# A decoder step on one core: rotary rows exchanged by small transfers, the spread of the sample gates two tiles later, small cache moves issued in other stages

## The reference, cut to what matters

```
mod = silu(c) @ w_ada + b_ada             # six shift / scale / gate vectors
h = rmsnorm(x) * (1 + scale1) + shift1
q, k, v, gates, q_dil, k_dil, v_dil, merge gates = split(h @ w_in)
rotate(x): first quarter of a head, half = d // 8
    out = [x1*cos - x2*sin, x2*cos + x1*sin, rest]     # x1, x2: its two halves
o_nsa = g0*compressed + g1*selected + g2*window attention
o_dil = three dilated groups, mixed by softmax weights
m = sigmoid(gA) * (o_nsa @ w_bn) + sigmoid(gB) * (o_dil @ w_bd)
x = x + gate1 * (m @ w_out)
x = x + gate2 * (silu(h2@w_gate) * (h2@w_up)) @ w_down
y = rmsnorm(x)
```

## Time and profile before

| what | value |
|---|---|
| median of three runs | 2079.82 us |
| the profiled execution | 2076.5 us, span 2074.7 us |
| PE busy | 1929.0 us, 93% of the span |
| DVE, ACT busy | 976.7 us, 772.7 us |
| granted TensorE clock, mean | 0.964 of full speed |
| DMA | 512.54 MB, mean 247 GB/s |
| chain that ended last | PE 84%, DMA 9%, DVE 4%, ACT 3% |

### The profile page before, as it was taken

The page is one execution under the profiler, slowest core; times in us unless marked ns, Lnnn a source line. Parts: engine busy times, 40 slices in busy tenths (PEclk is TensorE's granted clock), DMA queues, the critical chain, the costliest instruction groups (busy, mean ns, idle before and its releaser), DMA issues.

```text
span 2074.7 us, 36811 instructions
## 1 busy us (share of the span) xinstructions
PE 1929.0 (93%) x15765; PEld 1774.5 (86%) x15765; DVE 976.7 (47%) x1730; ACT 772.7 (37%) x1232; POOL 58.4 (3%) x108
## 2 busy tenths in 40 slices
PE   6988999999999987899999978999999999999967
PEld 3667999999755555799999968999999999999966
DVE  3355445554355532355445764444444333745424
ACT  2355333334344432443334334333333332633322
POOL 0000000000000000000000000000000000000010
PEclk9998989999999989799999989999999999999989
DMA  9981769899899855755656545676777766677791
GB/s 373 422 304 62 213 209 304 270 294 284 328 420 420 324 233 202 266 169 178 186 176 214 182 163 182 231 271 229 253 252 244 241 232 215 208 252 245 262 320 49
DMA packets 336138, 512.54 MB, mean 247 GB/s; under 512 B 8753, under 2 KB 310105, under 8 KB 319497
## 3 DMA queue, kind: packets, MB, share of 16 engines
q1 hardware_dynamic: 316146, 368.53, 53.0%
q0 software_dynamic: 5248, 125.73, 15.3%
q10 hardware_dynamic: 14640, 16.80, 2.5%
HBM read 504.29 MB, written 98.91 MB: 291 GB/s over the span
## 4 chain that ended last, share of the span: by engine, by line
PE 84%; DMA 9%; DVE 4%; ACT 3%; issue 1%; SPq 0%; DVEq 0%; ACTq 0%
PE bank L1132 18%; PE bank L1134 18%; PE bank L1133 18%; PE bank L845 5%; PE bank L846 5%; PE bank L847 5%; DMA piece<-in_w_ada 5%; PE bank L735 3%; PE bank L772 2%; DMA piece<-in_w_down 2%; PE bank L903 1%; DMA mem<-in_cache_sel_kv,runs 1%; PE bank L963 1%; PE bank L878 1%; PE bank L800 1%; DMA mem<-in_x_sample 1%
## 5 line engine op out<-in xcount | busy, mean ns | idle before, releaser
L1132 PE MATMUL bank<-piece,piece 128*128 128x264 f32 x3072 | 878.3, 286 | 49.3 <-DVE piece L2054 26.5
L1133 PE MATMUL bank<-piece,piece 128*128 128x264 f32 x3072 | 877.7, 286 | 0.0
L1134 PE MATMUL bank<-piece,piece 128*128 128x264 f32 x3072 | 877.4, 286 | 0.0
L2059 DVE TENSOR_TENSOR piece<-piece,piece 128x2048 fp32r<-128x2048 f32 (+2 forms) x216 | 440.8, 2053 | 504.0 <-ACT piece L1544 504.0
L1132 PEld LDWEIGHTS bank<-piece,piece 128*128 128x128 f32 x3072 | 583.2, 190 | 50.3 <-DVE piece L2059 22.7
L1544 ACT CAST piece<-piece 128x2048 fp32r<-128x2048 f32 (+2 forms) x216 | 368.8, 1715 | 588.3 <-PE bank L1134 509.6
L1134 PEld LDWEIGHTS bank<-piece,piece 128*128 128x128 f32 x3072 | 583.1, 190 | 0.0
L1133 PEld LDWEIGHTS bank<-piece,piece 128*128 128x128 f32 x3072 | 582.6, 190 | 0.0
L845 PE MATMUL bank<-piece,piece 128*128 128x264 f32 (+1 forms) x816 | 240.8, 295 | 0.0
L846 PE MATMUL bank<-piece,piece 128*128 128x264 f32 (+1 forms) x816 | 234.8, 288 | 0.0
L847 PE MATMUL bank<-piece,piece 128*128 128x264 f32 (+1 forms) x816 | 234.5, 287 | 0.0
(11 more groups left out here) (324 smaller groups left out, 1417.5 us busy)
## 6 DMA issues: line engine op xcount, KB each, us to landing
piece<-in_w_ada SPq DMA_DIRECT2D x48, 2048.0 KB, 12.9
out_s_dil<-in_cache_dil_kv POOLq DMA_DIRECT2D x64, 1023.5 KB, 6.2
piece<-in_w_in SPq DMA_DIRECT2D x50, 1024.0 KB, 8.1
piece<-in_w_gate SPq DMA_DIRECT2D x22, 2048.0 KB, 8.1
piece<-in_w_up SPq DMA_DIRECT2D x22, 2048.0 KB, 8.2
piece<-in_w_down SPq DMA_DIRECT2D x32, 1408.0 KB, 7.2
piece<-in_w_in SPq DMA_DIRECT2D x16, 2048.0 KB, 8.2
piece<-in_w_out SPq DMA_DIRECT2D x8, 2048.0 KB, 8.6
```

The source lines that it names most:

```text
L1132: mm(out, w_high[:, k, :], half_tile(x_high[k]), start=(start and k == first_tile), stop=False)
L1133: mm(out, w_high[:, k, :], half_tile(x_low[k]), start=False, stop=False)
L1134: last = mm(out, w_low[:, k, :], half_tile(x_high[k]), start=False, stop=(stop and k == len(x_high) - 1))
L2059: v.tensor_tensor(half_chunk(a, k_tiles, f, CW), raw, half_chunk(buffer, k_tiles).bitcast(F32), ALU.subtract)\
```

## The change

The rotary products of PE go. Each of the 35 rotated tiles has its rotary rows exchanged by transfers from `tmp` to one of two buffers (`swap0`, `swap1`, zero elsewhere), issued by SP: two transfers of 16 rows for a head of 128, four of 8 rows for two heads of 64, each row 1056 bytes. SP runs `swap(c - 4)` ahead of the load of chunk c; it waits for `raw` of that tile and for `roped` of the tile two earlier. DVE multiplies the exchanged rows by sin (whose table has the sign now) and adds one turn later, in `turned_half(n - 1)`, which waits for the transfers; the product with cos goes to a buffer that alternates. The two rotary matrices leave the first constants (256 words a row less), and the two zeroed buffers come with the rest of them (528 words more).

PE's spread of the sample gates moves from n = 1 to n = 3, into bank 5, and DVE's part of it from n = 1 to n = 4. On GpSimd, the copies of `dil2` come at one half of every merge turn, those of `dil1` and `win` at every second half of the output projection, and the second half of `dil3` last, with its waits as they were.

```diff
@@ -59,8 +59,8 @@
 CONST = {}
 S0 = "newmask"
 _c = 0
-for _n, _w in (("ident", P), ("rot_nsa", P), ("rot_dil", P), ("ones", P), ("part8", 8), ("cos_nsa", T), ("sin_nsa", T),
-               ("cos_dil", T), ("sin_dil", T), ("causal", 3 * P), ("dilmask", 9 * P),
+for _n, _w in (("ident", P), ("ones", P), ("part8", 8), ("cos_nsa", T), ("sin_nsa", T),
+               ("cos_dil", T), ("sin_dil", T), ("swap0", T), ("swap1", T), ("causal", 3 * P), ("dilmask", 9 * P),
                ("cmp_add", QT * NBP), ("cmp_mul", QT * NBP), ("rowsel", P), ("head_of", H),
                ("newmask", 64), ("new_dil", B), ("group", B * KVH), ("spread", P), ("keep", NSEL), ("force", NSEL),
                ("pick", 32), ("selmask", 4), ("pairof", 4), ("rowsel2", P), ("before", NSEL * NSEL)):
@@ -87,14 +87,11 @@
-        rot, cos, sin = np.zeros((P, P)), np.ones((P, T)), np.zeros((P, T))
+        cos, sin = np.ones((P, T)), np.zeros((P, T))
-                rot[base + i + half, base + i] = -1
-                rot[base + i, base + i + half] = 1
-                for r in (base + i, base + i + half):
-                    cos[r], sin[r] = np.cos(ang[:, i]), np.sin(ang[:, i])
-        put("rot_" + name, rot)
+                for r, sign in ((base + i, -1), (base + i + half, 1)):
+                    cos[r], sin[r] = np.cos(ang[:, i]), sign * np.sin(ang[:, i])
@@ -406,6 +403,8 @@
     def slot_at(s):
         return ring0 + s * SLOT if s < 3 else fourth
 
+    swapped = [const("swap0"), const("swap1")]
+    gate_parts = tmp[:, 3, 0:48]
     c_rows = mem[:, region:region + D]
     c_sig = facA.rearrange("p j c -> p (j c)")
     x_tm = mem[:, region + 2 * D:region + 4 * D].rearrange("p (q f) -> p q f", q=QT)
@@ -540,7 +540,23 @@
                 sp.wait_ge(*pe_.at("ada", a - 3))
             ada_load(a)
 
+        def swap(n):
+
+            if TILES[n][0] not in ROPED:
+                return
+            sp.wait_ge(*act_.at("raw", n))
+            if n >= 2 and TILES[n - 2][0] in ROPED:
+                sp.wait_ge(*dve_.at("roped", n - 2))
+            dh = DH if TILES[n][0] in "kq" else DD
+            for base in range(0, P, dh):
+                lo, hi = slice(base, base + dh // 8), slice(base + dh // 8, base + dh // 4)
+                sp.dma_start(swapped[n % 2][lo, :], tmp[hi, n % 3, :]).then_inc(*swap_in[n % 2].mark(by=16))
+                sp.dma_start(swapped[n % 2][hi, :], tmp[lo, n % 3, :])\
+                    .then_inc(*swap_in[n % 2].mark(*(("rows", n) if base + dh == P else ()), by=16))
+
         for c, (col, n) in enumerate(CHUNKS):
+            if c >= 4:
+                swap(c - 4)
             if c < 4:
                 sp.wait_ge(*pe_.at("ada", NA1 - 1 if c < 2 else NA1 - 3))
             else:
@@ -551,6 +567,8 @@
                 sp.wait_ge(*pe_.at("hid", "p"))
                 sp.dma_start(kcS.rearrange("p b n -> p (b n)"), kv_kept[:, 0:B * P]).then_inc(kv_loaded, 16)
                 sp.dma_start(vcS.rearrange("p b f -> p (b f)"), kv_kept[:, B * P:2 * B * P]).then_inc(kv_loaded, 16)
+        for n in range(NT - 4, NT):
+            swap(n)
         for a in range(NA1, NA1 + 3):
             sp.wait_ge(*pe_.at("acc", NT - 2 if a == NA1 else NT - 1))
             ada_load(a)
@@ -672,19 +690,19 @@
                 pool.wait_ge(*pe_.at("acc", 3 + (8 * c + eighth) * (NT - 4) // 32))
                 pool.dma_start(z, a).then_inc(*caches_copied.mark(by=16))
         selected_gathers()
+        for c in range(B):
+            for z, a in copies("dil2", 512, c):
+                pool.wait_ge(mg_half, 1 + 6 * c)
+                pool.dma_start(z, a).then_inc(*caches_copied.mark(by=16))
+        for c in range(B):
+            pool.wait_ge(wo_half, 1 + 2 * c)
+            for name, n in (("dil1", 128), ("win", WIN)):
+                for z, a in copies(name, n, c):
+                    pool.dma_start(z, a).then_inc(*caches_copied.mark(by=16))
         for c in range(B // 2, B):
             for eighth, (z, a) in enumerate(copies("dil3", 2048, c, 8)):
                 pool.wait_ge(ff_half, 2 + (8 * (c - B // 2) + eighth) * 84 // 32)
-                pool.dma_start(z, a).then_inc(*caches_copied.mark(by=16))
-        for c in range(B):
-            for z, a in copies("dil2", 512, c):
-                pool.wait_ge(dn_half, 1 + 7 * c)
-                pool.dma_start(z, a).then_inc(*caches_copied.mark(by=16))
-        for name, n in (("dil1", 128), ("win", WIN)):
-            for c in range(B):
-                for z, a in copies(name, n, c):
-                    pool.dma_start(z, a)\
-                        .then_inc(*caches_copied.mark(*(("all",) if (name, c) == ("win", B - 1) else ()), by=16))
+                pool.dma_start(z, a).then_inc(*caches_copied.mark(*(("all",) if (c, eighth) == (B - 1, 7) else ()), by=16))
 
 
     @block.tensor
@@ -790,16 +808,6 @@
             if x in (ADA_STEPS, NA1):
                 ada_turn(x // ADA_STEPS - 1)
 
-        def rope(n):
-            kind = TILES[n][0]
-            if kind not in ROPED:
-                return
-            pe.wait_ge(*act_.at("raw", n))
-            if n >= 2:
-                pe.wait_ge(*dve_.at("rope_bank", n))
-            mm(bank[4 + n % 2][:, 0:T], const("rot_nsa" if kind in "kq" else "rot_dil"), tmp[:, n % 3, :],
-               start=True, stop=True).then_inc(*pe_.mark("rot", n))
-
         def source(n):
             kind, j = TILES[n]
             return {"k": lambda: kT[:, j, :], "dk": lambda: dqk[:, DHEADS + j, :]}.get(kind, lambda: tmp[:, n % 3, :])()
@@ -852,12 +860,11 @@
                 for q in range(QT):
                     turn(bank[6][:, q * 48:(q + 1) * 48], tmp[0:48, 0, q * P:(q + 1) * P], ident[0:48, 0:48])
                 turn(bank[6][0:B, 128:176], tmp[0:48, 0, TP:T], ident[0:48, 0:48]).then_inc(*pe_.mark("gateT"))
+            if n == 3:
                 pe.wait_ge(*act_.at("gateS"))
                 pe.wait_ge(const_rest, 16)
-                mm(bank[7][:, 0:48], const("rowsel")[0:B, :], gates8[0:B, :], start=True, stop=True)\
+                mm(bank[5][:, 0:48], const("rowsel")[0:B, :], gates8[0:B, :], start=True, stop=True)\
                     .then_inc(*pe_.mark("gateS"))
-            if 1 <= n <= NT:
-                rope(n - 1)
             if n >= 2:
                 token_major(n - 2)
 
@@ -1779,7 +1786,28 @@
             v.tensor_tensor(hS, hS, modT[:, shift * KT:(shift + 1) * KT, 1:9], ALU.add).then_inc(*dve_.mark("h", tag))
 
         dve.wait_ge(const_rest, 16)
-        roped = []
+        def turned_half(n):
+
+            kind, j = TILES[n]
+            dve.wait_ge(*swap_in[n % 2].at("rows", n))
+            v.tensor_tensor(swapped[n % 2], swapped[n % 2], const("sin_nsa" if kind in "kq" else "sin_dil"), ALU.mult)\
+                .then_inc(*dve_.mark())
+            dve.wait_ge(*dve_.last())
+            if kind == "q":
+                kv = j // 4
+                for odd in range(2):
+                    r = slice(odd * DH, (odd + 1) * DH)
+                    last = v.tensor_tensor(qK[kv * DH:(kv + 1) * DH, (2 * j + odd) % G, :], rt[r, n % 2, :], swapped[n % 2][r, :], ALU.add)
+                    last.then_inc(*dve_.mark(*(("roped", n) if odd else ())))
+            else:
+                dst = {"k": lambda: kT[:, j, :], "dq": lambda: dqk[:, j, :], "dk": lambda: dqk[:, DHEADS + j, :]}[kind]()
+                v.tensor_tensor(dst, rt[:, n % 2, :], swapped[n % 2], ALU.add).then_inc(*dve_.mark("roped", n))
+            if n == 1:
+                dve.wait_ge(*dve_.last())
+                for h, l in PARTS:
+                    v.tensor_copy(kTcP[l * DH:(l + 1) * DH, h, :], kT[h * DH:(h + 1) * DH, 0, 0:TP].rearrange("p (m l) -> p l m", l=2)[:, l, :])\
+                        .then_inc(*dve_.mark())
+
         for n in range(NT):
             kind, j = TILES[n]
             if n + 2 < NT:
@@ -1799,40 +1827,21 @@
             if n == 13:
                 dve.wait_ge(*pe_.at("kvc", "p"))
                 v.tensor_copy(vcP[0:NBP, :], bank[6][0:NBP, P:2 * P]).then_inc(*dve_.mark("kvc", "p"))
-            if n == 1:
+            if n and TILES[n - 1][0] in ROPED:
+                turned_half(n - 1)
+            if n == 4:
                 dve.wait_ge(*pe_.at("gateS"))
-                g48 = rt[:, 0, 0:48].rearrange("p (j h) -> p j h", j=3)
-                link(v.tensor_tensor(g48, bank[7][:, 0:48].rearrange("p (j h) -> p j h", j=3),
+                g48 = gate_parts.rearrange("p (j h) -> p j h", j=3)
+                link(v.tensor_tensor(g48, bank[5][:, 0:48].rearrange("p (j h) -> p j h", j=3),
                                      const("head_of").unsqueeze(1).broadcast_to([P, 3, H]), ALU.mult))
                 link(v.tensor_reduce(gatesS, g48, AX.X, ALU.add))
             if kind not in ROPED:
                 continue
-            c = "nsa" if kind in "kq" else "dil"
             dve.wait_ge(*act_.at("raw", n))
-            if roped:
-                dve.wait_ge(*dve_.at("roped", roped[-1]))
```

(36 more changed lines are left out.)

## The result

The changed kernel takes 2059.13 us (median of 5 runs, 2054.17 to 2063.12) against 2079.82 us; the ratio is 0.9898, with a 95% interval of 0.9876 to 0.9921. It is faster, but by half of what was forecast (2038), and outside the range. The profiled execution has a span of 2057.3 us, 17.4 less than before.

What follows compares the result with a forecast made beforehand. PE was taken as the bound nearly everywhere; 15.4 (products) + 5.5 (gates) + 20.4 (end) = 41.3 us off a profiled 2076.5 gave 2035.2, and with 3.3 for the runs' median 2038 us was forecast, range 2031 to 2055.

Steps and rivals of the forecast that it cites:

- The end: Down projection: without the small copies a w_down load of 38.67 us takes 6 to 7; 20.4 us gained, lower clock included.
- The copies in their new stages: Merge and output projection: the moved cache copies fit in spare DMA time and cost 0.
- The gates: Projection: PE's wait of 3.69 us for ACT's sigmoids and 1.8 us of lower clock go; 5.5 us together.
- The rotary products: Projection: taking 35 products of 0.44 us off PE gains 15.4 us if PE stays the bound.
- The swaps: Projection: SP's wait and small issues delay loads, lateness of 0 to 0.7 us at most; priced at 0.
- the chance of a slower kernel: Whole kernel: 0.05 for slower than before, from rival (c) and a little of Rival (a) with clock losses.
- rival (c): Projection: SP's small issues are dear; 2152 us at 3.3 us an issue, slower than before from 1.5; chance 0.04.
- Rival (a): Projection: loads set the pace, DMA share 0.88 to 0.97, eating the products' 15.4 us; 2053 us; chance 0.13.
- The points that the prediction named against itself: Wrong if PE or casts wait for in_w_in, DVE for swaps, or the lower clock shows in merge or output projection.
- A slip without effect: Start: first constants shrink by 128 KB, second grow by 136; estimated 0.35 us, given back, taken as 0.
- The rule of the Trainium skill weighed in the prediction: Projection: a swap waits behind the load in flight, up to 2 to 4 us, landing at about 9, still ahead of DVE.

Runs made afterwards that it cites:

- e1: The kernel before with only the order of the cache copies changed; 2060.7 us, ratio 0.9914.
- e5: The kernel before with the new order of copies and the later spread of the gates, rotary products kept on PE; 2053.4 us, ratio 0.9883.
- e6: The changed kernel without the 32 cache copies of 1 MB that GpSimd issues during the projection; 2042.2 us, ratio 0.9813.
- e9: The changed kernel with each load issued ahead of the swaps and the projection's copies as 64 of 0.5 MB; 2040.9 us, ratio 0.9807.
- e2: The changed kernel with the load of chunk c issued ahead of swap(c - 4) instead of behind it; 2040.5 us, ratio 0.983.
- e7: The changed kernel with each swap transfer cut into two of half the rows, 184 issues instead of 92; 2082.4 us, ratio 1.0014.
- e8: The changed kernel with the projection's 32 copies of 1 MB as 64 of 0.5 MB; 2048.7 us, ratio 0.9861.
- e4: The changed kernel without the 92 swap transfers, SP's waits ahead of the loads kept; 2037.0 us, ratio 0.9799.
- e10: The load-first kernel (e2) unchanged, run again with more rounds; 2047.3 us, ratio 0.9836.

## Why the prediction was wrong

**The end: right.** 20.4 us forecast, 20.9 in the down projection and 19.4 by e1. The load of 38.67 us was the copies' doing. The burst held an issue on SP too. Of the three issues of w_down's loads from 1975 to 1991 us in the kernel before one took 20.3 us, and in e1 none of the 32 took over 0.383 (ns, min/median/max):

```profile
L612 SPq DMA_DIRECT2D piece<-in_w_down x3: 373/373/20305, 1975.2 to 1991.3; - x3
```

```profile
L612 SPq DMA_DIRECT2D piece<-in_w_down x32: 367/373/383, 1743.2 to 2010.6; - x32
```

**The copies in their new stages: right.** Merge, output projection and feed-forward took 894.2 us against 894.5. The 2 MB copies land in 8.3 us and the loads beside them in 9.0 (median), where they took 8.2. The output projection came to a share of 0.85, not the 0.79 of the sum (9.2 of 11.7 us), and PE was as busy.

**The gates: right in mechanism, a little too small.** 5.5 forecast, 6.8 measured by e5.

**The rotary products: right, but not to be had in this order.** With the loads on time for PE the stage takes 324.6 (e6, e9) to 326.8 us (e2). The forecast comes to 345.2 - 15.4 - 5.5 = 324.3. Against e5, which has the products, it is 338.4 - 324.6 = 13.8 us: the 15.4 was a little too much, as the gates' 5.5 was too little.

**The swaps: the step that failed.** "An issue on SP takes 0.367 us, so the load of chunk n+4 is issued at 3.2 (dilated heads) to 3.9 us (q, k)". It was issued at 6.1 and 8.3 on average, and the lateness that the sum put at 0 cost 18.2 us (342.5 against the forecast 324.3). Three things are in it.

The first is the plain price of an issue. One of 8 or 16 rows takes 0.51 to 0.77 us (median 0.62) where nothing holds it. The number of rows is not all of it, since the issue of the 128-row load behind the swaps is slower too, with a median of 0.58 us instead of 0.367:

```profile
L564 SPq DMA_DIRECT2D piece<-in_w_in x51: 367/582/5813, 133.5 to 526.1; - x51
```

In e6, where hardly an issue is held, the loads go out at 5.1 (q) and 3.7 us (dilated), so the plain price is 1.2 and 0.5 us of the lateness. The second is the holds: one issue in five takes over 1 us. Here is one tile of the changed kernel on SP, with GpSimd's last issue ahead of it (start us, us).

```profile
425.14 0.51 SPq L553 DMA_DIRECT2D mem<-mem  x1
425.69 2.79 SPq L554 DMA_DIRECT2D mem<-mem  x1
428.52 0.58 SPq L564 DMA_DIRECT2D piece<-in_w_in  x1
```

```profile
422.70 0.49 POOL L691 DMA_DIRECT2D out_s_dil<-in_cache_dil_kv  x1 [8.09 <-PE bank L855]
```

The second swap is held for 2.79 us, to 5.8 us after the copy's issue, and the load goes out at 428.5, where PE's tile had ended at 422.4. With 92 issues and 87.5 us in all, the mean is 0.95 us; a tile's swaps take 3.5 us (q) and 2.15 (dilated) instead of the 1.5 and 0.7 of the prediction. The third is the loop of the section on the result: the first swap starts 4.7 us (q) and 3.9 (dilated) after the tile's end on average, where the prediction had 2.45 and e6 has 2.3, because the raw copy stands behind a cast that waits for a late load. Of the 18 dilated loads whose landing the trace has, 10 landed more than 13.3 us after the tile's end (11.7 of two tiles, 1.6 of slack); in e2 and e6 none did.

On PE the 18 us are waits of 10.5 us for weights and 4.2 for rotated tiles, and about 3.4 us of the lower clock: among the tiles of dilated q and k 44 products start 0.22 us apart instead of 0.12, against 9 in e6. The prediction counted clock losses in the chance of a slower kernel and put nothing of them in the sum.

The prediction had the issues as rival (c), with a loss of 40s - 18 us for an issue of s, and gave it 4 in 100 because it took the median of another kind of transfer for s. At s = 0.95 the formula says 20 us, against 18.2. e7, with 184 issues of 0.86 us (s = 1.72 for a pair), makes it 51 us, and 371.0 - 324.3 = 46.7 was measured.

The agreement of the sums is in part luck. By the formula half of the 20 us falls on the 8 q tiles; measured, by the times between first products, they took 60.1 us against 61.7 in e6 and lost nothing, and the 24 dilated q and k tiles lost 17.7 (161.3 against 143.6), where the formula has 10. In e7 the q tiles lost 6.0 against 22 by the formula, the dilated ones 29.8 against 28. PE has 64 other products behind the third q tile (11.3 us in the kernel before), and late loads can catch up there; that this is why q lost nothing was not tried. So the rival had the right cause and the right loop, and not the right account by tiles.

Rival (a), to which 13 in 100 went, had the right symptom by another cause: loads set the pace since they were issued late, not since the engines were full. The points that the prediction named against itself, casts that wait for `in_w_in`, are what the profile shows.

A slip without effect: the second constants grow by 264 KB (528 words in 128 rows), and 136 is what both together grow by.

The rule of the Trainium skill weighed in the prediction ("DMA: Bandwidth & Descriptors", "Queues, rings and completion order": descriptors of one queue are consumed in ring order) did not decide. In e2 each swap stands behind a load issued just before it, where the rule bites hardest, and DVE waits 16.8 us for swaps in all, with 1.7 us of waits on PE.

**What stays open.** Why an issue is held while a copy moves was not tried. The 18 us are parted only roughly: e8 gives 12 of them back with shorter holds and landings that are no shorter; the waits of SP with the copies beside, and no issues, cost 2 (e4, 326.5 against 324.6 in e6); the plain price of the issues without the copies costs nothing (e6). The plain price with the copies beside but without holds has no run. Nor does any run show what held the issues of e2 that began after the copy had landed.

## What to carry to other kernels

When transfers join a queue that prefetches, put the prefetch ahead of them: it needs an old event, they need a new one, and the order on the queue makes the old one wait for the new. Look also for the way back, by which a late prefetch makes the new event late. Price an issue by one of the same shape, behind another issue and with the same traffic beside it, and multiply by the count: here the count, not the bytes, decided (e7). A burst of unhurried copies at the end of a kernel can cost as much as a large change elsewhere; spread over stages with DMA time to spare they cost nothing that could be measured here.

## What the runs showed of the hardware that was not expected

An issue on SP or ACT can be held while a DRAM-to-DRAM copy issued by GpSimd is moving, whichever of the two queues it goes through. With the swaps ahead of the loads a swap's issue took up to 3.6 us beside copies of 1 MB and up to 2.3 beside 0.5 MB, and 3 of 92 took over 1 us with none. With the loads ahead of the swaps it took up to 6.4 (e2) and 7.0 us (e10) beside 1 MB and 4.3 beside 0.5 MB (e9), and 8 of the 39 slow ones in e2 began after the last copy had landed, so a copy on the move is not the only thing that goes with a slow issue. Beside the 16 small copies at the end of the kernel before one issue took 20.3 us.

A transfer of 8 or 16 rows from SBUF to SBUF takes 0.51 to 0.77 us to issue where it is not held, against 0.37 for one of 128 rows from DRAM that stands alone on its queue and 0.58 for the same one behind two or four small ones.
